# Forgetting attention: plain f32 matmuls replaced by three rounded products of high and low parts

## The chip, the cores and the metric

The kernel runs on one core of a Trainium2 chip. The metric is device time in microseconds (us), the median of several runs. One run of the same program is also taken with the hardware profiler; its page and its trace are what is read here.

## What is computed

Two network blocks on a sequence of 512 tokens of width 1024, all in f32. The first block has two layers; the first of these is the one that is changed here. It projects the input to queries, keys and values of 12 heads of width 128, and attends causally, with a forget gate that adds a bias to each score:

```python
s = jnp.einsum('bhqd,bhkd->bhqk', qi, k).astype(jnp.float32) * scale
s = s + ci[..., None] - c[:, :, None, :]
mask = key_pos[None, :] <= qpos[:, None]
s = jnp.where(mask[None, None], s, NEG)
p = jax.nn.softmax(s, axis=-1).astype(v.dtype)
return jnp.einsum('bhqk,bhkd->bhqd', p, v)
```

Around it stand a cross attention with 4 heads over 256 memory rows, a gate `silu(z)` and an output projection. The second layer replaces the forgetting attention by retention. The second block (dilated attention, a convolution, a gated feed forward part) is not touched.

## The kernel before

Each engine has its own instruction stream, written by hand in the order in which it runs; engines wait for each other by semaphores (`x.wait_ge(semaphore, value)`). Nothing is scheduled by a planner.

**Two kinds of matmul.** A projection (`products`, L1845 to L1852) splits both its operands: weights and activations are rounded to fp32r ("high", `whi`, `Hh`), and what the rounding lost is rounded again ("low", `wlo`, `Hl`). Each 128-row chunk is then three matmuls on rounded operands, high times high, high times low and low times high, 128 x 512 each; a block has 8 chunks. The matmuls inside the attention (L1936 for the scores, L1969 for the weighted values) take plain f32 operands. TensorE runs each plain f32 matmul of the program as two MATMUL instructions, so the 48 of L1936 stand in the trace as 96. A transpose (L1952) is one.

**Weights.** SyncE loads a block of weights of 512 KB into one of 4 slots (L457), when the block four places earlier has been used. ScalarE rounds it (`whi`, L665), GpSimd subtracts (`wlo`, L531).

**The forgetting layer.** After the block for the forget gate and the first head's three blocks (q, k, z), 12 blocks (`val0`, L2094 to L2096) make the values of all heads, in three groups of four PSUM banks. ScalarE scales each bank and keeps it in `values` (`keep_values`, L831). Then there is one turn for each head i = 1 to 11 (`softmax_turn("fox", ...)`), each of about 22 us. TensorE runs in a turn:

1. `fox_scores` of head i-1: four matmuls, query block 0 to 3 against 128, 256, 384 and 512 keys, into the banks A0 to A3;
2. the q block and the k block of head i (`products`, 24 matmuls each);
3. `turn_probs`: 10 transposes of the probabilities of head i-1, again into A0 to A3;
4. the z block of head i; ahead of its fifth chunk (`c == 4`) stands `weigh_values` of head i-1: four matmuls of 512, 384, 256 and 128 columns, added up in the bank PV.

VectorE runs in a turn: the softmax of head i-1 (L1296 to L1313), q and k of head i out of PSUM (L1352, L1354), `head_out` (the weighted values times the gate, L1328, L1330, L1332), z of head i (L1357). ScalarE runs: the rounding of one block of weights, the exponentials (L740), the rounding of a second block, the copy of the transposed probabilities to `probsT` (L747, four copies), the rounding of a third block, tanh of z. The scores of head 11 and its weighted values stand in the first turn of the cross attention (`mem0`), where the weighted values come behind the fourth block.

## Time and profile before

| | us |
|---|---|
| median of 3 runs | 1866.2 |
| lowest, highest | 1865.28, 1867.84 |
| span of the profiled execution | 1865.8 |

The page of the profile gives busy time by engine, shares of the span in 40 slices, the chain of work that ended last, and groups of instructions by line. "PE" is TensorE's matmul, "PEld" its weight load, DVE is VectorE, ACT ScalarE, POOL GpSimd. Matmuls are pipelined: one that is shown as 0.39 us long may start 0.23 us after the one before it. What a matmul costs is therefore read from the distance of starts in the timeline, and not from its duration. Times in the timeline are from the start of the span.

### The profile page before, as it was taken

The numbers are of one execution on the slowest core, as the hardware profiler recorded it, in microseconds if no ns is written. First come the engines' busy times: TensorE is split into PE (matmuls) and PEld (weight loads), VectorE is DVE, ScalarE is ACT, GpSimd is POOL, SyncE is SP. The second block draws the span as 40 slices with busy tenths as digits, with TensorE's granted clock in tenths as the row PEclk, the third lists the DMA queues.
The fourth block names the chain that finished last, engine by engine and source line by source line (L and its number), as shares of the span: only waits on it lengthen the run. The fifth ranks groups of instructions, "written<-read, shape, count | busy, mean of one in ns | idle before, by whom it ended". The sixth has DMA issues, their size and how long they took to land.

```text
span 1865.8 us, 23617 instructions
## 1 busy us (share of the span) xinstructions
PE 1832.0 (98%) x8424; PEld 1498.3 (80%) x8424; DVE 847.1 (45%) x1494; ACT 735.5 (39%) x1159; POOL 786.2 (42%) x376
## 2 busy tenths in 40 slices
PE   8999999999999999999999999997999899999998
PEld 6887777888888777888888888885888678888887
DVE  5024334453110555534249988946333464455202
ACT  5333333333333565543343233347233374444313
POOL 3443344444444333443444444353444454444442
PEclk9999999999999999999999999999999999999999
DMA  5333332333333323333333433331333323333332
GB/s 169 109 85 86 90 90 80 91 96 90 91 96 108 101 80 91 89 92 90 96 96 91 108 95 80 80 79 44 92 101 102 90 76 92 92 101 91 112 96 96
DMA packets 293549, 174.20 MB, mean 93 GB/s; under 512 B 16368, under 2 KB 280072, under 8 KB 293472
## 3 DMA queue, kind: packets, MB, share of 16 engines
q1 hardware_dynamic: 280528, 165.17, 31.1%
q0 software_dynamic: 2448, 7.93, 1.7%
q10 hardware_dynamic: 10496, 0.07, 0.3%
q8 instruction: 49, 0.80, 0.2%
q14 instruction: 28, 0.23, 0.1%
HBM read 170.95 MB, written 2.20 MB: 93 GB/s over the span
## 4 chain that ended last, share of the span: by engine, by line
PE 93%; DMA 2%; DVE 2%; ACT 2%; issue 0%; POOL 0%; SPq 0%; DVEq 0%; ACTq 0%; POOLq 0%
PE proj L1849 22%; PE proj L1851 22%; PE proj L1850 22%; PE A L1936 1%; PE PV L1969 1%; PE A L2094 1%; PE A L2096 1%; PE A L2095 1%; PE A L2376 1%; PE A L2374 1%; PE A L2375 1%; DMA wraw<-w_in 1%; PE PV L1973 1%; PE A L1942 1%; PE A L1952 1%; PE A L2032 1%
## 5 line engine op out<-in xcount | busy, mean ns | idle before, releaser
L531 POOL TENSOR_TENSOR wlo<-wraw,whi 128x1024 fp32r<-128x1024 f32 (+1 forms) x305 | 723.2, 2373 | 1006.8 <-ACT whi L665 1006.3
L665 ACT ACTIVATE whi<-wraw 128x1024 fp32r<-128x1024 f32 (+1 forms) x304 | 318.5, 1048 | 770.0 <-DMA wraw<-w_in 179.0
L1849 PE MATMUL proj<-Hh,whi 128*128 128x512 f32 x1448 | 581.5, 402 | 0.5 <-DVE uv L1785 0.3
L1851 PE MATMUL proj<-Hh,wlo 128*128 128x512 f32 x1448 | 565.6, 391 | 0.0
L1850 PE MATMUL proj<-Hl,whi 128*128 128x512 f32 x1448 | 565.0, 390 | 0.0
L1849 PEld LDWEIGHTS proj<-Hh,whi 128*128 128x128 f32 x1448 | 272.6, 188 | 61.4 <-issue 4.3
L1850 PEld LDWEIGHTS proj<-Hl,whi 128*128 128x128 f32 x1448 | 272.7, 188 | 59.5 <-issue 5.0
L1851 PEld LDWEIGHTS proj<-Hh,wlo 128*128 128x128 f32 x1448 | 272.3, 188 | 58.0
L1532 DVE SCALAR_TENSOR_TENSOR A<-cin,dwT,A 128x512 f32<-128x512 f32 x232 | 175.1, 755 | 6.8
L1849 PE MATMUL proj<-Oh,whi 128*128 128x512 f32 x256 | 101.1, 395 | 0.8 <-DVE Ol L1332 0.8
L1850 PE MATMUL proj<-Ol,whi 128*128 128x512 f32 x256 | 99.7, 389 | 0.0
L1851 PE MATMUL proj<-Oh,wlo 128*128 128x512 f32 x256 | 99.7, 389 | 0.0
L1849 PEld LDWEIGHTS proj<-Oh,whi 128*128 128x128 f32 x256 | 48.1, 188 | 11.6 <-DVE Ol L1332 1.2
L1850 PEld LDWEIGHTS proj<-Ol,whi 128*128 128x128 f32 x256 | 48.1, 188 | 10.2 <-issue 0.5
L1851 PEld LDWEIGHTS proj<-Oh,wlo 128*128 128x128 f32 x256 | 48.0, 188 | 10.1
L1444 DVE TENSOR_TENSOR X<-X,proj 128x512 f32 (+1 forms) x16 | 11.0, 688 | 92.1 <-PE proj L1851 92.1
L1785 DVE TENSOR_TENSOR uv<-proj,rms 128x512 f32<-128x512 f32 x21 | 14.5, 692 | 81.8 <-PE proj L1851 81.8
L1328 DVE SCALAR_TENSOR_TENSOR ob<-PV,gate 128x512 f32<-128x512 f32 x20 | 13.8, 692 | 82.7 <-PE PV L1969 59.8
L1823 DVE TENSOR_TENSOR VT<-VT,gains 128x512 f32<-128x512 f32 x1 | 0.7, 700 | 101.2 <-ACT sq L1181 101.2
L756 ACT ACTIVATE ztanh<-z 128x512 f32<-128x512 f32 x20 | 12.6, 630 | 68.1 <-DVE z L1357 50.5
L1309 DVE RECIPROCAL small<-small 128x4 f32<-128x4 f32 x20 | 3.6, 178 | 77.3 <-ACT probs L740 77.3
L1668 DVE TENSOR_TENSOR sq<-proj,rms 128x512 f32<-128x512 f32 x16 | 11.1, 692 | 59.5 <-PE proj L1851 55.9
(440 smaller groups left out, 2799.5 us busy)
## 6 DMA issues: line engine op xcount, KB each, us to landing
wraw<-w_in SPq DMA_DIRECT2D x68, 512.0 KB, 3.8
wraw<-fox_w_in SPq DMA_DIRECT2D x57, 512.0 KB, 3.7
wraw<-ret_w_in SPq DMA_DIRECT2D x44, 512.0 KB, 3.8
wraw<-w_up SPq DMA_DIRECT2D x44, 512.0 KB, 3.8
wraw<-w_out SPq DMA_DIRECT2D x40, 512.0 KB, 4.0
wraw<-w_down SPq DMA_DIRECT2D x22, 512.0 KB, 3.6
wraw<-w_mem_kv SPq DMA_DIRECT2D x16, 512.0 KB, 4.1
wraw<-conv_pw_w SPq DMA_DIRECT2D x8, 512.0 KB, 4.0
```

Source lines behind the costliest of these rows:

```text
L531: pool.tensor_tensor(wlo[s][:, 0:r, :], wraw[s][:, 0:r, :], whi[s][:, 0:r, :].bitcast(F32), ALU.subtract).then_inc(w_lo, 1)
L665: f(whi[s][:, 0:r, :], wraw[s][:, 0:r, :], ACT.Copy).then_inc(w_hi, 1)
L1532: ins = stt(conv_sum if tap < CONV - 1 else C[:, c, :], cin[:, c, tap:tap + S], dwT[:, c * CONV + tap:c * CONV + tap + 1], conv_sum, ALU.m ...
L1849: mm(dst, whi[s][:, c, :], xh, start=(first and c == 0), stop=False)
L1850: mm(dst, whi[s][:, c, :], xl, start=False, stop=False)
L1851: ins = mm(dst, wlo[s][:, c, :], xh, start=False, stop=(last and c == chunks - 1))
L1936: mm(A[i][:, 0:w], q[:, i * P:(i + 1) * P], k[:, 0:w], start=True, stop=True).then_inc(scores, 1)
L1942: mm(A[j][:, 0:NMEM], qm[:, j * P:(j + 1) * P], km, start=True, stop=True).then_inc(scores, 1)
L1952: ins = pe.transpose(A[j][:, (i - j) * P:(i - j + 1) * P], probs[:, FOXAT[i] + j * P:FOXAT[i] + (j + 1) * P], ident[:])
L1969: ins = mm(PV[:, j * P:S], values[:, u, j * P:(j + 1) * P], probsT[:, TRI[j]:TRI[j] + S - j * P], start=(j == 0), stop=(j == NT - 1))
L1973: ins = mm(PV[:], vtok[0][:, j, :], probsT[:, j * S:(j + 1) * S], start=(j == 0), stop=(j == MT - 1))
L2032: ins = mm(ret_sum[e][:, j * P:S], values[:, r, j * P:(j + 1) * P], decayed[e][:, TRI[j]:TRI[j] + S - j * P], start=(j == 0), stop=(j == N ...
```

## The change

In the 12 heads of the forgetting layer, every operand of the scores and of the weighted values is held as a high and a low part in fp32r, and each plain f32 matmul becomes three rounded ones. One stays: the scores of query block 0 (128 x 128). The high parts of q, k and of the probabilities are made by ScalarE (the copy to `probsT` writes `probs_high` in its stead), the low parts by VectorE. The values are kept as `Oh` and `Ol`, in place of `values`. Then `weigh_values` stands ahead of the seventh chunk of the z block instead of the fifth. The two tables `rcos` and `rsin` of the retention are loaded behind the cross attention, not at the start, since `probs_low` lies over them.

The core of the diff:

```diff
+        q_high, k_high, q_low = r_high[0], r_high[1], r_low[1]
...
@@ -547,8 +562,6 @@
                         split("val0", 0, b)
                     pool.wait_ge(b_out, 2)
                     pool.dma_start(b_dram, bias_rows[:]).then_inc(b_stored, 16)
-                    pool.dma_start(rcos[:], t["c_cos"]).then_inc(in_rope, 16)
-                    pool.dma_start(rsin[:], t["c_sin"]).then_inc(in_rope, 16)
                     pool.wait_ge(c_ready, 1)
                     pool.dma_start(c_dram, f_b).then_inc(c_stored, 16)
                     pool.wait_ge(c_stored, 16)
@@ -588,6 +601,9 @@
             for i in range(1, HEADS):
                 fox_turn(i)
             turns("mem0")
+            pool.wait_ge(pv_done, HEADS)
+            pool.dma_start(rcos[:], t["c_cos"]).then_inc(in_rope, 16)
+            pool.dma_start(rsin[:], t["c_sin"]).then_inc(in_rope, 16)
             turns("wo0")
             for b in range(HEADS):
                 split("val1", 0, b)
@@ -744,7 +760,9 @@
                 act.wait_ge(turned, u + 1)
                 if kind == "fox":
                     for j in range(NT):
-                        ins = f(probsT[:, TRI[j]:TRI[j] + S - j * P], A[j][:, 0:S - j * P], ACT.Copy)
+                        ins = f(probs_high[:, TRI[j]:TRI[j] + S - j * P], A[j][:, 0:S - j * P], ACT.Copy)
+                        if j < NT - 1:
+                            ins.then_inc(p_high, 1)
                 else:
                     for j in range(MT):
                         ins = f(probsT[:, j * S:(j + 1) * S], A[j][:], ACT.Copy)
@@ -762,6 +780,11 @@
             FOXW, FOXAT = [P * (i + 1) for i in range(NT)], [0, 128, 384, 768]
             MEMW, MEMAT = [NMEM] * NT, [NMEM * i for i in range(NT)]
 
+            def high_of(i, b):
+
+                act.wait_ge(evac, PH["fox"].g(i, b) + 1)
+                f((q_high, k_high)[b][:], (q, k)[b][:], ACT.Copy).then_inc(qk_high_made, 1)
+
             def softmax_turn(name, i, u, before):
 
                 if before == "ret":
@@ -770,6 +793,8 @@
                     split(name, i, 0, i)
                     exps(u - 1, FOXW, FOXAT)
                     split(name, i, 1, i)
+                    high_of(i, 0)
+                    high_of(i, 1)
                     copy_probsT(u - 1, before)
                     split(name, i, 2, i)
                     z_and_v(name, i, u)
@@ -828,7 +853,8 @@
                         act.wait_ge(v_summed[L], (NT - 1) * group + j + 1)
                     else:
                         act.wait_ge(w_used, PH["val" + str(L)].n(0, 4 * group + 3) + 1)
-                    f(kept_values(group, j), v_banks[L][group][j][:].rearrange("p (h n) -> p h n", h=4), ACT.Identity,
+                    to = kept_values(group, j) if L else split_values(group, j)[0]
+                    f(to, v_banks[L][group][j][:].rearrange("p (h n) -> p h n", h=4), ACT.Identity,
                       scale=(x_roots, v_roots)[L][:, j:j + 1]).then_inc(v_kept[L], 1)
 
             def value_turns(L):
@@ -839,6 +865,9 @@
                     if L == 0 and b < 2:
                         for c in range(4 * b, 4 * b + 4):
                             mem_high(c)
+                    if L == 0 and b == 2:
+                        high_of(0, 0)
+                        high_of(0, 1)
                 keep_values(L, 2)
 
             def ret_finish(i):
@@ -1283,6 +1312,35 @@
             for c in range(KC):
                 mem_low(c)
 
+            def low_of(i, b):
+
+                dve.wait_ge(qk_high_made, 2 * i + b + 1)
+                tt((q_low, k_low)[b][:], (q, k)[b][:], (q_high, k_high)[b][:].bitcast(F32), ALU.subtract).then_inc(qk_low_made, 1)
+
+            def low_values(group):
+
+                for j in range(NT):
+                    high, low = split_values(group, j)
+                    dve.wait_ge(v_kept[0], NT * group + j + 1)
+                    stt(low, v_banks[0][group][j][:].rearrange("p (h n) -> p h n", h=4), x_roots[:, j:j + 1],
+                        high.bitcast(F32), ALU.mult, ALU.subtract).then_inc(v_low, 1)
+
+            def low_probs(u):
+
+                for j in range(NT):
+                    if j < NT - 1:
+                        dve.wait_ge(p_high, (NT - 1) * u + j + 1)
+                    else:
+                        dve.wait_ge(probs_out, u + 1)
+                    at = slice(TRI[j], TRI[j] + S - j * P)
+                    ins = tt(probs_low[:, at], A[j][:, 0:S - j * P], probs_high[:, at].bitcast(F32), ALU.subtract)
+                ins.then_inc(p_low, 1)
+
+            low_of(0, 0)
+            low_of(0, 1)
+            for group in range(GROUPS):
+                low_values(group)
+
             def softmax(u, widths, at):
 
                 if widths is FOXW:
@@ -1352,6 +1410,9 @@
                     stt(q[:], proj[ph.bank(0, i)][:], SCALE, rms[:], ALU.mult, ALU.mult).then_inc(evac, 1)
                     arrived(name, i, 1)
                     tt(k[:], proj[ph.bank(1, i)][:], rms[:], ALU.mult).then_inc(evac, 1)
+                    low_of(i, 0)
+                    low_of(i, 1)
+                    low_probs(u - 1)
                     head_out(u - 1, head)
                     arrived(name, i, 2)
                     tt(z[0][:], proj[ph.bank(2, i)][:], rms[:], ALU.mult).then_inc(evac, 1)
@@ -1365,6 +1426,8 @@
                 dve.tensor_copy(vT[:, 0:NMEM], proj[ph.bank(2)][:, 0:NMEM]).then_inc(evac, 1)
                 if before in ("fox", "mem") and not late:
                     head_out(u - 1, head)
+                if late:
+                    low_probs(u - 1)
                 arrived(name, i, 3)
                 tt(z[0][:], proj[ph.bank(3)][:], rms[:], ALU.mult).then_inc(evac, 1)
                 if late:
@@ -1929,11 +1992,14 @@
             def fox_scores(u):
 
 
-                pe.wait_ge(evac, PH["fox"].g(u, 1) + 1)
-                since(pe, probs_out, u)
-                for i in range(NT):
-                    w = P * (i + 1)
-                    mm(A[i][:, 0:w], q[:, i * P:(i + 1) * P], k[:, 0:w], start=True, stop=True).then_inc(scores, 1)
+                pe.wait_ge(qk_low_made, 2 * u + 2)
+                since(pe, p_low, u)
+                mm(A[0][:, 0:P], q[:, 0:P], k[:, 0:P], start=True, stop=True).then_inc(scores, 1)
+                for i in range(1, NT):
+                    to, at, w = A[i][:, 0:P * (i + 1)], slice(i * P, (i + 1) * P), P * (i + 1)
+                    mm(to, q_high[:, at], k_high[:, 0:w], start=True, stop=False)
+                    mm(to, q_high[:, at], k_low[:, 0:w], start=False, stop=False)
+                    mm(to, q_low[:, at], k_high[:, 0:w], start=False, stop=True).then_inc(scores, 1)
 
             def mem_scores(name, i, u):
                 pe.wait_ge(evac, PH[name].g(i, 1) + 1)
@@ -1959,15 +2025,19 @@
                 ins.then_inc(turned, 1)
 
             def weigh_values(u, kind):
-                pe.wait_ge(probs_out, u + 1)
-                if kind == "mem":
+                if kind == "fox":
+                    pe.wait_ge(p_low, u + 1)
+                else:
+                    pe.wait_ge(probs_out, u + 1)
                     pe.wait_ge(v_out, u - HEADS + 1)
 
                 since(pe, o_done, u)
                 if kind == "fox":
                     for j in range(NT):
-                        ins = mm(PV[:, j * P:S], values[:, u, j * P:(j + 1) * P], probsT[:, TRI[j]:TRI[j] + S - j * P],
-                                 start=(j == 0), stop=(j == NT - 1))
+                        to, of, at = PV[:, j * P:S], slice(j * P, (j + 1) * P), slice(TRI[j], TRI[j] + S - j * P)
+                        mm(to, Oh[:, u, of], probs_high[:, at], start=(j == 0), stop=False)
+                        mm(to, Oh[:, u, of], probs_low[:, at], start=False, stop=False)
+                        ins = mm(to, Ol[:, u, of], probs_high[:, at], start=False, stop=(j == NT - 1))
                 else:
                     for j in range(MT):
                         ins = mm(PV[:], vtok[0][:, j, :], probsT[:, j * S:(j + 1) * S], start=(j == 0), stop=(j == MT - 1))
@@ -1987,11 +2057,11 @@
                 if name == "fox":
                     fox_scores(u - 1)
                     if i == 1:
-                        pe.wait_ge(v_kept[0], HEADS)
+                        pe.wait_ge(v_low, HEADS)
                     products(name, i, 0, 0, H, par=i)
                     products(name, i, 1, 1, H, par=i)
                     turn_probs(u - 1, before)
-                    products(name, i, 2, 2, H, par=i, each=lambda c: weigh_values(u - 1, before) if c == 4 else None)
+                    products(name, i, 2, 2, H, par=i, each=lambda c: weigh_values(u - 1, before) if c == 6 else None)
                     return
                 if before == "fox":
                     fox_scores(u - 1)
@@ -2105,7 +2175,7 @@
                 if b == 4:
                     pe.wait_ge(mem_lo, KC)
                 if b == 8:
-                    pe.wait_ge(v_kept[0], 4)
+                    pe.wait_ge(v_low, 4)
                 values_of(0, b)
                 if b == 0:
                     pe.wait_ge(mem_scaled, MT)
@@ -2116,7 +2186,7 @@
                     for x in range(4, KC):
                         pe.wait_ge(mem_lo, x - 3)
                         turn_mem(x)
-            pe.wait_ge(v_kept[0], 8)
+            pe.wait_ge(v_low, 8)
             for i in range(1, HEADS):
                 softmax_turn("fox", i, i, "fox")
 
```

**On TensorE, the weighted values of one head and the scores of the next.** In a row before, the four matmuls of the weighted values, in the middle of the z block, and the four of the scores, between two blocks:

```order
L1969 MATMUL PV<-probsT,values 128x512 [waits o_done,probs_out]
L1969 MATMUL PV<-probsT,values 128x384
L1969 MATMUL PV<-probsT,values 128x256
L1969 MATMUL PV<-probsT,values 128x128
...
L1936 MATMUL A<-k,q 128x128 [waits probs_out,evac]
L1936 MATMUL A<-k,q 128x256
L1936 MATMUL A<-k,q 128x384
L1936 MATMUL A<-k,q 128x512
```

and now:

```order
L2038 MATMUL PV<-probs_high,Oh 128x256
L2039 MATMUL PV<-probs_low,Oh 128x256
L2040 MATMUL PV<-probs_high,Ol 128x256
L2038 MATMUL PV<-probs_high,Oh 128x128
L2039 MATMUL PV<-probs_low,Oh 128x128
L2040 MATMUL PV<-probs_high,Ol 128x128
...
L1997 MATMUL A<-k,q 128x128 [waits p_low,qk_low_made]
L2000 MATMUL A<-r_high 128x256
L2001 MATMUL A<-k_low,r_high 128x256
L2002 MATMUL A<-r_high,r_low 128x256
```

Eight plain matmuls have become one plain and 21 rounded ones. (`r_high` is the name under which q_high and k_high lie, `r_low` that of q_low.)

**On VectorE, between k of a head and the output of the head before.** Before:

```order
L1354 TENSOR_TENSOR k<-proj,rms 128x512 [waits w_used]
L1328 SCALAR_TENSOR_TENSOR ob<-PV,gate 128x512 [waits gated,pv_done]
L1330 CAST Oh<-ob 128x512 [waits o_done]
L1332 TENSOR_TENSOR Ol<-ob,Oh 128x512 [waits dve_own]
```

and now:

```order
L1412 TENSOR_TENSOR k<-proj,rms 128x512 [waits w_used]
L1318 TENSOR_TENSOR r_low<-q,r_high 128x512 [waits qk_high_made]
L1318 TENSOR_TENSOR k_low<-k,r_high 128x512 [waits qk_high_made]
L1336 TENSOR_TENSOR probs_low<-A,probs_high 128x512 [waits p_high]
L1336 TENSOR_TENSOR probs_low<-A,probs_high 128x384 [waits p_high]
L1336 TENSOR_TENSOR probs_low<-A,probs_high 128x256 [waits p_high]
L1336 TENSOR_TENSOR probs_low<-A,probs_high 128x128 [waits probs_out]
L1386 SCALAR_TENSOR_TENSOR ob<-PV,gate 128x512 [waits gated,pv_done]
```

Six subtractions have come in between; the first two wait for ScalarE's rounding of q and k, the next three for a copy of the probabilities each, and the sixth for the last copy (`probs_out`).

**On ScalarE, at the same place.** Before:

```order
L665 ACTIVATE whi<-wraw 128x1024 [waits w_used,w_landed0]
L747 ACTIVATE probsT<-A 128x512 [waits turned]
L747 ACTIVATE probsT<-A 128x384
L747 ACTIVATE probsT<-A 128x256
L747 ACTIVATE probsT<-A 128x128
L665 ACTIVATE whi<-wraw 128x1024 [waits w_used,w_landed1]
```

and now:

```order
L681 ACTIVATE whi<-wraw 128x1024 [waits w_used,w_landed0]
L786 ACTIVATE r_high<-q 128x512 [waits evac]
L786 ACTIVATE r_high<-k 128x512 [waits evac]
L763 ACTIVATE probs_high<-A 128x512 [waits turned]
L763 ACTIVATE probs_high<-A 128x384
L763 ACTIVATE probs_high<-A 128x256
L763 ACTIVATE probs_high<-A 128x128
L681 ACTIVATE whi<-wraw 128x1024 [waits w_used,w_landed1]
```

The rounding of q and of k stands between the rounding of a block of weights and the four copies of the probabilities, which are the same as before but for the tile they write.

## Rows read from the trace of the kernel before

**Rows 1.** The page: busy us, share of the span, instructions; and the chain.

```profile
PE 1832.0 (98%) x8424; PEld 1498.3 (80%) x8424; DVE 847.1 (45%) x1494; ACT 735.5 (39%) x1159; POOL 786.2 (42%) x376
...
PE 93%; DMA 2%; DVE 2%; ACT 2%; issue 0%; POOL 0%; SPq 0%; DVEq 0%; ACTq 0%; POOLq 0%
```

**Rows 2.** Waits, 100 to 360 us (who <- for whom: total, times, longest).

```profile
PEld proj L1849 <- ACT values L831: 0.5, 1, 0.5
```

**Rows 3.** The turns of the heads: busy us (PE PEld DVE ACT POOL), granted clock.

```profile
110.00:352.00 242.00, 242.00 (x1087) 191.51 (x1087) 98.43 (x313) 83.12 (x180) 100.08 (x56) 1.00 0.32 84
```

**Rows 4.** Timeline, TensorE, scores of one head: start, length, engine, instruction.

```profile
219.47 2.32 PE L1936 MATMUL A<-k,q 128*128 128x128 f32 x8
...
221.87 0.40 PE L1850 MATMUL proj<-Hl,whi 128*128 128x512 f32 x1
```

**Rows 5.** Timeline, TensorE, transposes and weighted values of a head.

```profile
210.72 1.25 PE L1952 MATMUL A<-ident,probs 128*128 128x128 f32 x10
...
212.05 0.39 PE L1850 MATMUL proj<-Hl,whi 128*128 128x512 f32 x1
...
214.57 2.32 PE L1969 MATMUL PV<-probsT,values 128*128 128x512 f32 x8
...
216.95 0.39 PE L1850 MATMUL proj<-Hl,whi 128*128 128x512 f32 x1
```

**Rows 6.** Timeline, TensorE, first and last of 48 rounded matmuls of 256 columns.

```profile
358.16 0.28 PE L1849 MATMUL proj<-Mh,whi 128*128 128x256 f32 x1
...
363.79 0.28 PE L1851 MATMUL proj<-Mh,wlo 128*128 128x256 f32 x1
```

**Rows 7.** Timeline, end of the value blocks: ScalarE keeps, TensorE goes on.

```profile
110.28 2.32 PE L1936 MATMUL A<-k,q 128*128 128x128 f32 x8
110.37 0.68 ACT L831 ACTIVATE values<-PV,small 128x512 f32<-128x512 f32 x1
...
110.94 1.27 ACT L831 ACTIVATE values<-proj,small 128x512 f32<-128x512 f32 x2
...
112.67 0.39 PE L1850 MATMUL proj<-Hl,whi 128*128 128x512 f32 x1
```

**Rows 8.** Timeline, turn 6: k ends, rounding, copies, weighted values.

```profile
232.33 0.39 PE L1851 MATMUL proj<-Hh,wlo 128*128 128x512 f32 x1
...
232.84 1.06 ACT L665 ACTIVATE whi<-wraw 128x1024 fp32r<-128x1024 f32 x1 [6.04 <-DMA wraw<-fox_w_in]
...
233.85 1.43 ACT L747 ACTIVATE probsT<-A 128x512 f32<-128x512 f32 x4
...
236.18 0.41 PEld L1969 LDWEIGHTS PV<-probsT,values 128*128 128x128 f32 x2
...
236.41 2.32 PE L1969 MATMUL PV<-probsT,values 128*128 128x512 f32 x8
```

**Rows 9.** Timeline, turn 7, the same places.

```profile
254.98 1.06 ACT L665 ACTIVATE whi<-wraw 128x1024 fp32r<-128x1024 f32 x1 [6.46 <-DMA wraw<-fox_w_in]
...
258.25 2.32 PE L1969 MATMUL PV<-probsT,values 128*128 128x512 f32 x8
```

**Rows 10.** Timeline, VectorE, turn 6: z, three softmax steps, normalising.

```profile
219.67 0.69 DVE L1357 TENSOR_TENSOR z<-proj,rms 128x512 f32<-128x512 f32 x1 [0.45 <-PE proj L1851]
...
220.49 0.29 DVE L1296 CUSTOM_DVE_ANT_0 probs<-A,decay 128x128 f32<-128x128 f32 x1
...
221.12 0.42 DVE L1296 CUSTOM_DVE_ANT_0 probs<-A,decay 128x256 f32<-128x256 f32 x1
...
221.98 0.56 DVE L1296 CUSTOM_DVE_ANT_0 probs<-A,decay 128x384 f32<-128x384 f32 x1 [0.21 <-PE A L1936]
...
227.04 1.36 DVE L1313 TENSOR_SCALAR probs<-probs,small 128x128 f32<-128x128 f32 x4
```

**Rows 11.** Timeline, GpSimd, end of the cross attention, start of the output projection.

```profile
434.64 2.38 POOL L531 TENSOR_TENSOR wlo<-wraw,whi 128x1024 fp32r<-128x1024 f32 x1 [1.44 <-ACT whi L665]
442.22 2.41 POOL L531 TENSOR_TENSOR wlo<-wraw,whi 128x1024 fp32r<-128x1024 f32 x1 [5.20 <-ACT whi L665]
```

More of the change, by code:

```diff
@@ L174, in build @@
             probs = sb("probs", [P, 1280], F32, one)
+            with ExitStack() as halves:
+                probs_high = sb("probs_high", [P, 1280], F32R, halves)
             probsT = sb("probsT", [P, 1280], F32, one)
-            z = [sb(f"z{e}", [P, S], F32, one) for e in range(2)]
-            gate = [sb(f"gate{e}", [P, S], F32, one) for e in range(2)]
+            z0, gate0 = sb("z0", [P, S], F32, one), sb("gate0", [P, S], F32, one)
+            with ExitStack() as halves:
+                k_low = sb("k_low", [P, S], F32R, halves)
+            z1 = sb("z1", [P, S], F32, one)
+            with ExitStack() as halves:
+                probs_low = sb("probs_low", [P, 1280], F32R, halves)
+            gate1 = sb("gate1", [P, S], F32, one)
+            rcos = sb("rcos", [P, S], F32, one)
+            rsin = sb("rsin", [P, S], F32, one)
+            z, gate = (z0, z1), (gate0, gate1)
             with ExitStack() as squared:
@@ L182, in build @@
             decay = [sb(f"decay{e}", [P, S], F32, one) for e in range(2)]
-            rcos = sb("rcos", [P, S], F32, one)
-            rsin = sb("rsin", [P, S], F32, one)
             mean_r = sb("mean_r", [P, P], F32R, one)
@@ L298, in build @@
         turned, probs_out, pv_done, o_done = sem("turned"), sem("probs_out"), sem("pv_done"), sem("o_done")
+        qk_high_made, qk_low_made, p_high, p_low, v_low = (sem(x) for x in ("qk_high_made", "qk_low_made", "p_high", "p_low", "v_low"))
         v_turned, v_out, z_tanh, gated = sem("v_turned"), sem("v_out"), sem("z_tanh"), sem("gated")
@@ L439, in kept_values, with split_values @@
             return values[:, 4 * group:4 * group + 4, j * P:(j + 1) * P]
+        def split_values(group, j):
+            at = slice(4 * group, 4 * group + 4), slice(j * P, (j + 1) * P)
+            return Oh[:, at[0], at[1]], Ol[:, at[0], at[1]]
         block = ctx.enter_context(nc.Block())
```

## Prediction

> **What bounds the kernel now.** I read the page first: TensorE is busy for 98% of the span and is 93% of the chain that ended last [rows 1]. Then the waits over all the turns of the forgetting layer. In 260 us TensorE waits for another engine once, for 0.5 us, behind the values that ScalarE keeps [rows 2], and its clock is granted in full [rows 3], so 2.4 GHz. VectorE is busy for 98 of 242 us there and ScalarE for 83 [rows 3]. So the time of this layer is the sum of what TensorE's instructions cost, and the cost of one is the distance of starts in the timeline. The change has two faces: shorter groups on TensorE, and longer chains on ScalarE and VectorE behind which TensorE could begin to wait.
>
> **Prices.** (a) Rounded, 512 columns: from 221.87 to 232.33 there are 46 steps [rows 4, 8], 0.227 us each. (b) Rounded, 256 columns: 47 steps from 358.16 to 363.79 [rows 6], 0.120 us. Columns over 2.4 GHz are 0.213 and 0.107, so both carry the same 0.013 us extra, and 384 columns should take 0.173. (c) The scores of a head in plain f32: from 219.47 to the next block's start, which is 221.87 less one step of 0.227, are 2.17 us [rows 4]. The weighted values, 214.57 to 216.95 less 0.227, are 2.15 [rows 5]. Both are 1280 columns in two instructions each, so 4 cycles a column. (d) A plain 128-column instruction: 10 transposes from 210.72 to 212.05 less 0.227 are 1.10 us, 0.11 each [rows 5]; a plain 128 x 128 matmul is two, 0.22.
>
> The profile's 4 cycles a column agree with the Trainium skill, FP8 and Floating Point Precision, section TensorE Precision Notes: true FP32 takes four passes. By passes alone the new form would save a quarter, 0.53 us a group of 2.13, 12.8 us in 24 groups, and 1855.0 after the waits below. The rows say less, for each rounded matmul carries its 0.013.
>
> **Scores, 12 heads.** Now 0.22 for block 0, then 3 x (0.120 + 0.173 + 0.227) = 1.56, and 0.02 at the change of kind as in (c): 1.80 against 2.17. Gain 0.37 x 12 = 4.4 us.
>
> **Weighted values, 12 heads.** The three wide widths are 1.56 again. Then come three rounded matmuls of 128 columns, a shape that the trace does not show. Bounds: the line through (a) and (b) gives 0.067 each; a full plain matmul of that width is 0.22 each, which it would be if rounding brought nothing for narrow ones. Between them stands the nearest row, the 128-column instruction of the transposes with a weight load of its own, 0.11. I take 0.11, as no instruction with its own weight load comes faster in these rows. The group is then 1.56 + 0.33 = 1.89 against 2.15: gain 0.26 x 12 = 3.1 us. With 0.067 it is 0.13 a head more, with 0.22 it is 0.33 a head less, 4.0 us in all.
>
> The Trainium skill, TensorE: Matmul & The Clock Gate, section LDWEIGHTS, gives a load of 128 columns 107 ns; an estimate by it would put three narrow ones at 0.32, where the line of the rows has 0.20. No run here shows this shape yet.
>
> **Start of the turns: a new wait.** The last value is kept by 110.94 + 1.27 = 112.21, and the q block behind the first scores starts at 112.67 less 0.227 = 112.44 [rows 7], 0.23 after it, one weight load. Now VectorE must also make the last low part of the values. Its steps of 512 columns take 0.69 with 0.60 from start to start, as fast as ScalarE's 0.57 [rows 7, 10], so it ends one step later: 112.21 + 0.04 + 0.69 = 112.94, and q starts at 113.17. The first scores would be through at 110.28 + 1.80 = 112.08. TensorE loses 1.1 us, once. The first softmax begins 2 us later on VectorE; that is covered, since the normalised probabilities are there at 228.40 in turn 6 and wanted by the transposes at 232.56 [rows 8, 10], 4.2 us of slack.
>
> **The chain to the weighted values, 11 turns.** In turn 6, ScalarE rounds weights from 232.84 [rows 8], and an instruction hands over 0.10 before its end (110.37 to 110.94 for a length of 0.68 [rows 7]). So q is rounded from 233.80, k from 234.37, and the copies, 1.43 long in all, end at 236.37 instead of 235.28. VectorE takes k's low part from 235.04, then the four of the probabilities. Their widths cost 0.69, 0.56, 0.42 and 0.29, by z and by the softmax steps that also read a bank and SBUF [rows 10], each less 0.09 when in a row. They end at 237.33. The weighted values now stand two chunks later, 6 x 0.227: from 236.41 to 237.77, their weight load from 236.18 to 237.54 [rows 8]. Slack 0.21 us: the two chunks just about pay for the chain. In turn 7 the rounding starts at 254.98 and the weighted values at 258.25 [rows 9]: the chain of 4.49 ends at 259.47, the load is due at 259.38, late by 0.09. By the same working turn 1 is even, the others have 0.1 to 0.5, one 1.8. Since I built this chain out of eight neighbours' durations, I take 0.5 us in sum, with bounds of 0 and 3.
>
> **What costs nothing.** The low parts of q and k for the scores are ready by 235.6, the scores come at 241. The later `head_out` moves z's copy some 0.5 us back; its bank is wanted a whole block of 5.4 us later. The softmax starts 0.5 us later by it, within the 4.2 us. VectorE gets 1.3 + 2.0 us more a turn, ScalarE 1.2, in turns of 21.8, at busy shares of 41% and 34% [rows 3]. In the first turn of the cross attention the weighted values come a whole block behind the transposes, which covers the chain. The tables' load moves into a hole of 5.2 us on GpSimd [rows 11]: two issues, and 0.5 MB beside a weight block that is used three blocks later. Where it stood before, TensorE waited for no weights.
>
> **Sum.** 4.4 + 3.1 - 1.1 - 0.5 = 5.9 us. The profiled execution's 1865.8 becomes 1859.9; it lies 0.4 under the median, so 1860.3.
>
> **Rivals.**
> - *Narrow rounded matmuls are dear.* Three at 0.22 eat up the gain of the weighted values: 0.66 + 1.56 = 2.22 against 2.15. Then 5.9 - 4.0 = 1.9 us are left: 1864.3, which can't be told from no change. For it: nothing in the trace is rounded and narrower than 256 columns, so nothing excludes it. Against it: (a) and (b) show rounded matmuls at one cycle a column at either width.
> - *They are as cheap as the line says.* 1.5 us more: 1858.8. Against it: there is no start-to-start distance under 0.11 here with a fresh weight load; but none was asked for by a rounded one.
> - *The chain comes late and the change costs time.* The place is the first weight load of the weighted values, which waits for `p_low`. ScalarE's two roundings stand between a landing weight block and the copies, and VectorE's low parts of q and k stand ahead of those of the probabilities. Each 0.1 us of lateness costs 1.1 us. With the other terms at 6.4, the sum is zero at 0.6 us late in each of 11 turns, and slower by 0.2% at 0.9 us. It takes a weight block that lands 1 us later in a turn, or 0.12 us more on each of eight instructions. At 1 us late: 1866.2 - 6.4 + 11 = 1870.8. Against it: the landing hangs on TensorE's own blocks and moves with them; in turns 6 and 7 it lies 0.28 and 0.58 behind k's end [rows 8, 9].
>
> **How the numbers follow.** Forecast 40% (1860.3), dear narrow ones 28% (1864.3), cheap ones 18% (1858.8), a late chain 14%: 3% still faster, 5% with the gain gone, 6% slower. A measurement of this kernel can tell about 0.2%, 3.7 us, from no change: faster means under 1862.5. Faster: 0.40 + 0.18 + 0.03 = 0.61; same: 0.28 + 0.05 = 0.33; slower 0.06. The range goes from 1857.8, the cheap case with no wait, to 1865.0, the dear case with half a us of extra waits.
>
> **What would show it.** In the profile of the changed kernel: scores of 1.80 us from their first start to the next block; weighted values of 1.89, and the starts of their last three at 0.11, 0.067 or 0.22; one wait of about 1 us ahead of the q block at 112; 0 to 0.1 us a turn ahead of the weighted values, by VectorE. Wrong would be: a wait in every turn at that place, a wait of the scores, or a turn that is longer though its groups are shorter.

## The result, and the profile after

| | kernel before | changed kernel |
|---|---|---|
| time, median (lowest to highest) | 1865.74 us (1862.6 to 1867.84, 4 runs) | 1887.64 us (1885.44 to 1888.39, 4 runs) |
| ratio to before, 95% interval | | 1.0115 (1.0101 to 1.0128) |
| span of the profiled execution | 1865.8 us | 1885.6 us |
| one turn of the heads (mean of 11) | 21.84 us | 23.64 us |

The change costs 1.15%, where I had forecast a gain of 0.3%. The page of the changed kernel, busy times and the chain by engine, against [rows 1]:

```profile
PE 1833.5 (97%) x8508; PEld 1510.9 (80%) x8508; DVE 909.0 (48%) x1578; ACT 747.5 (40%) x1183; POOL 793.8 (42%) x376
...
PE 86%; DVE 5%; DMA 4%; ACT 3%; issue 1%; POOL 0%; SPq 0%; DVEq 0%; ACTq 0%; POOLq 0%
```

The busy shares hardly move. The chain does: TensorE's share falls from 93% to 86%, VectorE's rises from 2% to 5%. So something on VectorE now sets the pace for a part of the time. TensorE's waits in the turns of the heads, where [rows 2] had one of 0.5 us (total, times, longest):

```profile
PE PV L2038 <- DVE probs_low L1336: 19.3, 11, 2.2
...
PE proj L1912 <- DVE Ol L1325: 1.1, 1, 1.1
```

In every one of the 11 turns TensorE stands ahead of the weighted values until VectorE has made the low part of the probabilities, 1.75 us each time. Measured from the first matmul of a head's scores to the next head's, a turn was 21.84 us, eleven times (240.2 us). It is now 23.91, 23.01, 22.95, 23.16, 25.07, 23.39, 23.73, 24.92, 23.36, 23.45 and 23.05 (260.0 us). The eleven turns are taken off the spans, and 1625.6 us are left of either (1865.8 - 240.2 and 1885.6 - 260.0). So the whole loss, 19.8 us, lies in the turns.

Turn 6 of the changed kernel, the chain to the weighted values (timeline of all engines; compare [rows 8]):

```profile
241.17 1.06 ACT L681 ACTIVATE whi<-wraw 128x1024 fp32r<-128x1024 f32 x1 [5.17 <-DMA wraw<-fox_w_in]
...
242.13 0.62 ACT L786 ACTIVATE r_high<-q 128x512 fp32r<-128x512 f32 x1
242.31 2.40 POOL L546 TENSOR_TENSOR wlo<-wraw,whi 128x1024 fp32r<-128x1024 f32 x1 [5.53 <-ACT whi L681]
...
242.65 0.62 ACT L786 ACTIVATE r_high<-k 128x512 fp32r<-128x512 f32 x1
...
242.78 2.48 DVE L1318 TENSOR_TENSOR r_low<-q,r_high 128x512 fp32r<-128x512 f32 x1 [0.54 <-ACT r_high L786]
...
243.18 1.40 ACT L763 ACTIVATE probs_high<-A 128x512 fp32r<-128x512 f32 x4
...
244.68 1.74 POOL L582 TENSOR_TENSOR decay<-decay,sq 128x512 f32<-128x512 f32 x1
...
245.18 1.78 DVE L1318 TENSOR_TENSOR k_low<-k,r_high 128x512 fp32r<-128x512 f32 x1
...
246.43 2.76 POOL L546 TENSOR_TENSOR wlo<-wraw,whi 128x1024 fp32r<-128x1024 f32 x1
...
246.89 1.67 DVE L1336 TENSOR_TENSOR probs_low<-A,probs_high 128x512 fp32r<-128x512 f32 x4
...
248.61 0.50 PE L2038 MATMUL PV<-probs_high,Oh 128*128 128x512 f32 x1 [1.90 <-DVE probs_low L1336]
```

ScalarE is as forecast: its copies of the probabilities end 3.41 us after the rounding of the weights begins (forecast: 236.37 less 232.84, 3.53). VectorE is not. The low part of q takes 2.48 us and that of k 1.78, where I had 1.3 for the two together. The four low parts of the probabilities behind them take 1.67 together (forecast 1.69), although a subtraction of GpSimd runs beside them too.

The reader should look at the ends rather than at the lengths. The low part of q ends at 245.26, which is 0.55 after GpSimd's `wlo` (242.31 + 2.40 = 244.71). That of k ends at 246.96, 0.54 after GpSimd's addition into `decay` (244.68 + 1.74 = 246.42). That addition was issued while q's low part ran; alone it takes 1.28, here 1.74, and 245.26 + 1.28 is 0.12 more than its end. These are not two engines that share something and both get slower. Each time, the one that comes second does its work when the first has ended: VectorE's 0.69 us end 0.55 behind GpSimd, so all but about 0.14 of them lie behind it.

### The profile page after: what moved, and what is told of

Read it like the earlier page. It is cut to its first block, busy times and chain, and to the rows that moved or that the text cites. A ratio compares the mean times of both kernels' runs of the same rounds, so it can differ in the third digit from the quotient of the medians.

```text
span 1885.6 us, 23893 instructions
## 1 busy us (share of the span) xinstructions
PE 1833.5 (97%) x8508; PEld 1510.9 (80%) x8508; DVE 909.0 (48%) x1578; ACT 747.5 (40%) x1183; POOL 793.8 (42%) x376
## 4 chain that ended last, share of the span: by engine, by line
PE 86%; DVE 5%; DMA 4%; ACT 3%; issue 1%; POOL 0%; SPq 0%; DVEq 0%; ACTq 0%; POOLq 0%
PE proj L1912 21%; PE proj L1914 20%; PE proj L1913 20%; DMA wraw<-fox_w_in 2%; PE A L2164 1%; PE A L2165 1%; PE A L2166 1%; DVE r_low L1318 1%; PE A L2444 1%; PE A L2446 1%; PE A L2445 1%; DVE k_low L1318 1%; ACT whi L681 1%; DVE probs_low L1336 1%; PE PV L2043 1%
```

## The experiments

Theory A: VectorE's subtractions with both inputs in SBUF (`q`, `r_high`; `k`, `k_high`) cannot run beside a GpSimd instruction that reads SBUF, and the low parts of the probabilities stand behind them. Rival B: the chain is simply longer than its slack, whatever runs on GpSimd. Rival C: the wait is only half of the loss, and the other half is in the new shapes on TensorE or in its clock. All edits are made to the changed kernel. Each ratio below is to the kernel before, in runs on the same chip.

### 1. The low parts of the probabilities first

```diff
                     tt(k[:], proj[ph.bank(1, i)][:], rms[:], ALU.mult).then_inc(evac, 1)
+                    low_probs(u - 1)
                     low_of(i, 0)
                     low_of(i, 1)
-                    low_probs(u - 1)
```

> The changed kernel with one exchange on VectorE: the low parts of the probabilities are made ahead of the low parts of q and k, not behind them. Theory A (an instruction of VectorE with both inputs in SBUF stands still while GpSimd subtracts; one with an input in PSUM does not): the low parts of the probabilities end about 1 us before the weighted values are due, the wait of about 1.9 us in each of 11 turns is gone, and the kernel takes 1860 to 1863 us (q's and k's low parts now come close to the next scores). Rival B (the chain of roundings, copies and subtractions is too long by itself, whatever its order): at least 1 us of wait stays in a turn, 1875 us or more. Rival C (the loss lies in the rounded matmuls or the clock, not in the wait): 1887 us as now.

Measured: 1859.92 us (1857.82 to 1862.67, 6 runs; before 1866.15 in 20), ratio 0.997 (0.9958 to 0.9983). There is no wait ahead of the weighted values any more, and a turn is 21.19 us. VectorE and GpSimd in turn 6:

```profile
231.67 1.13 DVE L1318 TENSOR_TENSOR r_low<-q,r_high 128x512 fp32r<-128x512 f32 x1
...
232.72 0.68 DVE L1318 TENSOR_TENSOR k_low<-k,r_high 128x512 fp32r<-128x512 f32 x1
...
232.96 2.71 POOL L546 TENSOR_TENSOR wlo<-wraw,whi 128x1024 fp32r<-128x1024 f32 x1 [0.71 <-ACT whi L681]
```

The loss is gone with the place of two calls in VectorE's order, and no instruction is left out. The turn was forecast at 21.84 - 0.37 - 0.26 = 21.21, so both gains on TensorE are real. What VectorE does ahead of `low_probs` cost the 20 us, not what TensorE now executes. It does not tell A from B yet, since this order takes the two low parts out of the chain whatever they last. But the other direction of A is seen here: k's low part comes first and takes its 0.68, and GpSimd's `wlo`, which starts 0.24 later, takes 2.71 instead of 2.40. Nor are the two low parts quick in this order: q's lasts 1.13 behind GpSimd's addition (231.67), and in two turns k's meets `wlo` and lasts 2.88, longer than in the changed kernel. These turns take 21.19 us like the others, since nobody waits for k's low part there.

### 2. GpSimd reads nothing beside them

In the turns of the heads after the first, GpSimd fills `wlo` with zeros and does not subtract, so the low part of those weights is left out of the product.

```diff
                 pool.wait_ge(w_hi, n + 1)
+                if name == "fox" and i:
+                    pool.memset(wlo[s][:, 0:r, :].bitcast(F32), 0.0).then_inc(w_lo, 1)
+                    return
                 pool.tensor_tensor(wlo[s][:, 0:r, :], wraw[s][:, 0:r, :], ...
```

> The changed kernel, but in the head turns GpSimd fills the low part of the weights with zeros instead of subtracting (the low part of these weights is left out of the result). Its order and its waits stay, it only reads nothing from SBUF in these 33 instructions. Theory A: the low parts of q and k take 0.69 us each instead of 2.48 and 1.78, except where they meet the 1.3 us that GpSimd adds the mask; the wait of a turn falls from 1.9 us to between 0 and 1, 1860 to 1872 us. Rival B (GpSimd has nothing to do with it, the subtractions are slow since q and its high part are read together, or because ScalarE and TensorE read beside them): both stay at 2.5 and 1.8 us, and the time at 1887 us.

Measured: 1859.02 us (1857.77 to 1861.37, 8 runs), ratio 0.9964 (0.9953 to 0.9974). One wait of 0.5 us is left ahead of the weighted values. Turn 6 (lines are three higher, by the edit):

```profile
231.18 0.95 POOL L547 MEMSET wlo<- 128x1024 f32 x1 [6.21 <-ACT whi L684]
...
231.84 0.68 DVE L1321 TENSOR_TENSOR r_low<-q,r_high 128x512 fp32r<-128x512 f32 x1
...
232.09 1.58 POOL L585 TENSOR_TENSOR decay<-decay,sq 128x512 f32<-128x512 f32 x1
232.62 1.61 DVE L1321 TENSOR_TENSOR k_low<-k,r_high 128x512 fp32r<-128x512 f32 x1
```

This tells A from B. VectorE's order and TensorE's are those of the changed kernel, only GpSimd's instruction is another, and q's low part is back at 0.68 (median of 12: 0.681), though the fill overlaps it by 0.29. In the ten turns in which it follows the fill, the overlap is 0.15 to 0.46 us and the length never over 0.69. So a GpSimd instruction that only writes does not hold it up. k's low part still meets the addition and ends at 234.23, 0.56 after that one's end at 233.67. It is the same law with another partner.

### 3. q's parts early, k's still ahead of the probabilities

```diff
+                    high_of(i, 0)
                     split(name, i, 1, i)
-                    high_of(i, 0)
...
+                    low_of(i, 0)
                     arrived(name, i, 1)
                     tt(k[:], proj[ph.bank(1, i)][:], rms[:], ALU.mult).then_inc(evac, 1)
-                    low_of(i, 0)
```

> The changed kernel, with q rounded and its low part made right behind q, in a stretch in which GpSimd is idle; k's low part still stands ahead of the probabilities' and still meets GpSimd's subtraction. Theory A: q's low part takes 0.69 us; k's waits for the end of GpSimd's instruction and then takes 0.6 more; the probabilities' end some 0.6 us late, 0.5 to 0.8 us of wait in a turn, 1865 to 1869 us. Rival B (the number of instructions in the chain counts, 0.7 us each): two instructions of 1.2 us in sum are out of the chain, the wait falls from 1.9 to 0.7 us: nearly the same time, but k's low part takes 0.69 us and starts late. The durations tell them apart, the time does not.

Measured: 1863.06 us (1859.49 to 1866.83, 10 runs), ratio 0.999 (0.9978 to 1.0001). Turns are 21.3 to 22.1 us. Turn 6, and the wait over all turns:

```profile
227.79 0.69 DVE L1318 TENSOR_TENSOR r_low<-q,r_high 128x512 fp32r<-128x512 f32 x1 [0.70 <-ACT r_high L786]
...
230.29 2.39 POOL L546 TENSOR_TENSOR wlo<-wraw,whi 128x1024 fp32r<-128x1024 f32 x1 [5.21 <-ACT whi L681]
...
231.28 1.96 DVE L1318 TENSOR_TENSOR k_low<-k,r_high 128x512 fp32r<-128x512 f32 x1 [0.70 <-ACT r_high L786]
```

```profile
PE PV L2038 <- DVE probs_low L1336: 2.3, 7, 0.6
```

q's low part now runs where GpSimd is idle and takes 0.69. k's is the one that meets `wlo`, and its end is 233.24, again 0.56 after GpSimd's (232.68). The wait shrinks from 19.3 to 2.3 us in sum. That is less than the 0.5 to 0.8 a turn that I expected, and so is the time (1865 to 1869). At the weight load the wait is longer, as the load is due before the matmul: 6.5 us in sum or 0.59 a turn, against 23.9 in the changed kernel. The turns tell a little more than the waits do: they are longer than those of the next experiment by 0.46 us each (239.42 less 234.39, over 11), with 0.21 of it in the waits. Another 0.2 is what a late group costs beside the counted wait (0.3 in each of 7), which is taken up under "What the 20 us are".

### 4. Both moved: the order that the chain wants

q's parts early as in 3; of k, ScalarE's rounding behind the copies of the probabilities, and VectorE's low part behind theirs.

```diff
+                    high_of(i, 0)
                     split(name, i, 1, i)
-                    high_of(i, 0)
-                    high_of(i, 1)
                     copy_probsT(u - 1, before)
+                    high_of(i, 1)
...
+                    low_of(i, 0)
                     arrived(name, i, 1)
                     tt(k[:], proj[ph.bank(1, i)][:], rms[:], ALU.mult).then_inc(evac, 1)
-                    low_of(i, 0)
-                    low_of(i, 1)
                     low_probs(u - 1)
+                    low_of(i, 1)
```

> Both: q's high and low parts behind q, where GpSimd is idle, and k's high and low parts behind the copies and low parts of the probabilities. Theory A: no wait ahead of the weighted values, none ahead of the scores (k's low part is ready 1 us or more before them, even blocked), turns of 21.2 us instead of 21.84 before: 1859 to 1861 us, the forecast of the prediction without its 0.5 us. Rival B: with only the copies and four subtractions left in the chain this should be free of waits too, so it doesn't tell A from B; it tells what the shorter groups on TensorE are worth: if the gain of 7.5 us less 1.1 is not there, the prices were wrong.

Measured: 1859.69 us (1855.14 to 1860.09, 5 runs), ratio 0.9953 (0.9936 to 0.9969). Ten turns of 21.19 us and the first, with the wait at its start, of 22.50. VectorE and GpSimd:

```profile
231.55 2.40 POOL L546 TENSOR_TENSOR wlo<-wraw,whi 128x1024 fp32r<-128x1024 f32 x1 [5.77 <-ACT whi L681]
...
232.41 1.68 DVE L1336 TENSOR_TENSOR probs_low<-A,probs_high 128x512 fp32r<-128x512 f32 x4 [1.03 <-ACT probs_high L763]
...
233.91 1.29 POOL L582 TENSOR_TENSOR decay<-decay,sq 128x512 f32<-128x512 f32 x1
234.01 1.73 DVE L1318 TENSOR_TENSOR k_low<-k,r_high 128x512 fp32r<-128x512 f32 x1
```

Here both sides of the law stand in four rows. The low parts of the probabilities lie inside GpSimd's subtraction but for their last 0.14 us, and neither side takes longer than alone: 2.40 for GpSimd, and 1.68 against 1.67 in turn 6 of experiment 2, where no subtraction of GpSimd is beside them. Their first input is a bank of PSUM. k's low part has two inputs in SBUF; it starts 0.10 after the addition, the addition keeps its 1.29, and k's low part ends 0.54 after it. It still takes 1.73 us; only nobody waits for it now.

In the same profile, TensorE without a wait shows the prices of the new groups (weighted values from 235.69, scores from 238.97):

```profile
235.69 0.39 PE L2038 MATMUL PV<-probs_high,Oh 128*128 128x512 f32 x1
...
237.26 0.22 PE L2038 MATMUL PV<-probs_high,Oh 128*128 128x128 f32 x1
237.32 0.28 PE L2039 MATMUL PV<-probs_low,Oh 128*128 128x128 f32 x1
237.43 0.27 PE L2040 MATMUL PV<-probs_high,Ol 128*128 128x128 f32 x1
...
237.82 0.40 PE L1913 MATMUL proj<-Hl,whi 128*128 128x512 f32 x1
...
238.97 0.38 PE L1997 MATMUL A<-k,q 128*128 128x128 f32 x2
...
240.77 0.39 PE L1912 MATMUL proj<-Hh,whi 128*128 128x512 f32 x1
```

Scores: 1.80 us, forecast 1.80. Weighted values: 237.82 less one step of 0.227, less 235.69, are 1.90; forecast 1.89. The three narrow rounded matmuls take 0.33 in all (237.26 to 237.59), so 0.11 each, with starts 0.06 and 0.11 apart at first: the nearest row was the right price, and neither rival on the narrow ones came.

### 5. The start of the turns

Experiment 4, and the last group of values takes its banks in another order, so that q's bank is among the first to be read out; TensorE then waits for ten low parts, not twelve.

```diff
-        v_banks = ((others, A, others), (A, others, A))
+        v_banks = ((others, A, (*proj, VT, PV)), (A, others, A))
...
-                        pe.wait_ge(v_low, HEADS)
+                        pe.wait_ge(v_low, 2 * NT + 2)
```

> The reordered kernel (e4) with the third group of values laid into the banks in another order: the two that the next q and k blocks write come first, so that TensorE waits for 10 of the 12 low parts of the values instead of all. The prediction put 1.1 us on this wait, and e4 shows 1.0. If that is its whole cause, the wait is gone and nothing takes its place, since q would start behind the scores at about the time at which the tenth low part is ready (within 0.2 us): 0.8 to 1.0 us under e4, so 1858.7 to 1859. If VectorE's first softmax, which begins behind the twelfth as before, becomes late for the first transposes, the gain is given back: the time of e4.

Measured: 1855.06 us (1854.55 to 1859.71, 5 runs; before 1866.59 in 9), ratio 0.9945 (0.9931 to 0.9959). The first turn is 21.20 us instead of 22.50. It starts thus:

```profile
107.43 1.41 DVE L1325 SCALAR_TENSOR_TENSOR Ol<-proj,small,Oh 128x512 fp32r<-128x512 f32 x2 [19.15 <-ACT Oh L857]
...
108.76 0.74 DVE L1325 SCALAR_TENSOR_TENSOR Ol<-VT,small,Oh 128x512 fp32r<-128x512 f32 x1
...
108.99 0.40 PE L1912 MATMUL proj<-Hh,whi 128*128 128x512 f32 x1
```

The two low parts of the `proj` banks are made by 108.84, and q's block follows the scores with no wait. The changed kernel has the same places with a wait of 1.07:

```profile
112.10 1.40 DVE L1325 SCALAR_TENSOR_TENSOR Ol<-proj,small,Oh 128x512 fp32r<-128x512 f32 x2
...
113.56 0.49 PE L1912 MATMUL proj<-Hh,whi 128*128 128x512 f32 x1 [1.07 <-DVE Ol L1325]
```

That was forecast as 1.1, once, so this term held. This kernel is faster than the kernel before and the changed one. The turn accounts for 1.3 us against experiment 4. Most of the remaining 3.3 us between the two medians is not owed to the edit: in the profiled executions the first scores start at 107.2 here and at 110.5 in experiment 4. The other profiles fall on one side or the other too: 107.6 to 107.9 in experiments 1, 3 and 6, 110.0 to 110.5 in the kernel before, both profiles of the changed kernel and experiment 2.

Most of that difference arises in the first 16 us. In the profile of experiment 4, two rounded matmuls of 512 columns start 0.42 us apart (13.76 and 14.18), which is one column a cycle at 1.2 GHz. Here the same two are 0.24 apart (12.87 and 13.11), at 2.4 GHz. From 12 to 15 us TensorE does 22 or 23 matmuls in the four profiles with the early scores and 12 or 13 in the five with the late ones. (The column of the granted clock has 1.00 in both, so it is the steps that tell.) Why the fast level comes some 5 us later in some executions stays open. The times of whole runs carry this difference of about 3 us in their starts, the lengths of the turns do not. Experiment 4's own runs fall in two groups, 1855.1 to 1855.3 and 1859.7 to 1860.1, and those of experiment 5 in 1854.6 to 1855.2 and one of 1859.7. Group by group their means differ by 0.3 us or less, so the 1.3 us of the first turn are shown by the trace and not by the times.

### 6. The weighted values one chunk later

The wait alone is made shorter: TensorE does three more matmuls, 0.68 us, ahead of the group.

```diff
-                    products(..., each=lambda c: weigh_values(u - 1, before) if c == 6 else None)
+                    products(..., each=lambda c: weigh_values(u - 1, before) if c == 7 else None)
```

> The changed kernel with the weighted values one chunk (0.68 us) further back in the z block. If the low parts come at a fixed time behind k, and TensorE stands idle until then, each turn is 0.68 us shorter: 11 x 0.68 = 7.5 us, from 1887.6 to 1880. If the wait moves along with TensorE's place, nothing changes. If the long turns (25.1 and 24.9 us against 23.3 of the others), in which the granted clock fell, come from the length of the wait, they are gone too, another 3.4 us: 1876.7.

Measured: 1876.15 us (1872.36 to 1877.15, 4 runs), ratio 1.0049 (1.0033 to 1.0064), 11.5 us less than the changed kernel. The wait over all turns, and the clock of all turns (the last columns of the window are granted clock, DMA share, GB/s):

```profile
PE PV L2038 <- DVE probs_low L1336: 12.8, 11, 1.3
```

```profile
110.00:365.00 255.00, 241.44 (x1179) 201.72 (x1180) 156.99 (x392) 94.74 (x206) 106.84 (x56) 1.00 0.30 81
```

The turns are 250.4 us in sum, 9.6 less than in the first profile of the changed kernel. The waits give 6.5 of it (19.3 less 12.8), 0.59 a turn. The other 3.1 are the two long turns, which are not there: none is over 22.8 us but the first, 23.88. Of the 11.5 us, the rest is mostly the start: this profile's first scores come at 107.6, those of the changed kernel at 110.5.

### 7. The changed kernel again

> The changed kernel once more, on the chip of the two others. In its first profile two turns of the eleven took 25.07 and 24.92 us where the others took 23.0 to 23.9, and the granted clock was lower in these two. If something in those turns causes it, the same two are long again. If it is the clock that falls behind a wait of 2 us in some turns and not in others, other turns, or another number of them, are long. Time 1885 to 1889 us either way.

Measured: 1887.8 us (1883.78 to 1888.63, 4 runs), ratio 1.0109 (1.0093 to 1.0124): the result stands. The turns are 24.39, 23.47, 23.26, 23.31, 23.19, 25.30, 23.57, 23.39, 23.23, 25.20 and 23.51 us. Its waits, and the stretch with the sixth turn:

```profile
PE PV L2038 <- DVE probs_low L1336: 21.1, 11, 2.3
```

```profile
228.00:252.00 24.00, 21.73 (x100) 18.21 (x100) 12.96 (x34) 8.35 (x18) 9.76 (x5) 0.93 0.28 77
```

There are two long turns again, but the sixth and tenth, not the fifth and eighth. So they aren't tied to a place in the program.

### The long turns

In the first profile of the changed kernel, the stretch with the fifth turn and the one behind it:

```profile
205.00:228.00 23.00, 20.95 (x95) 17.46 (x94) 12.17 (x32) 8.20 (x18) 9.70 (x5) 0.93 0.30 80
228.00:252.00 24.00, 22.10 (x109) 18.45 (x108) 14.15 (x36) 8.34 (x18) 9.75 (x5) 1.00 0.29 77
```

And TensorE in the former, from the wait on:

```profile
223.69 0.50 PE L2038 MATMUL PV<-probs_high,Oh 128*128 128x512 f32 x1 [2.05 <-DVE probs_low L1336]
...
224.98 0.53 PE L2039 MATMUL PV<-probs_low,Oh 128*128 128x384 f32 x1
225.30 0.53 PE L2040 MATMUL PV<-probs_high,Ol 128*128 128x384 f32 x1
225.62 0.42 PE L2038 MATMUL PV<-probs_high,Oh 128*128 128x256 f32 x1
```

384 columns are 0.32 us apart, which is one column a cycle at 1.2 GHz; without the wait they are 0.17 apart. A turn less its wait is 21.46 to 21.49 us in eight of the eleven turns (the first, with the start wait, 22.84); in the fifth and eighth it is 23.02 and 23.04. The low clock therefore costs 1.55 us each time. It came in 4 of the 22 turns of the two profiles, behind waits of 2.05, 1.88, 2.27 and 2.16 us; others as long (2.25, 2.11) were not followed by it, and none of the 11 waits up to 1.33 of experiment 6 was. What decides within the long ones stays open.

## Why the prediction was wrong

**TensorE's terms held.** Scores 1.80 us (forecast 1.80), weighted values 1.90 (1.89), narrow rounded matmuls 0.11 each (0.11, nearest row), a turn without a wait 21.19 (21.21). The start wait is 1.07 (1.1). Experiments 1, 2 and 4, with no wait ahead of the weighted values or one of 0.5 us, come to 1859.9, 1859.0 and 1859.7, where the forecast for the changed kernel was 1860.3. It is the time of a kernel whose low parts of the probabilities are not held up (and the start of the program alone moves these times by 3 us, so the agreement is no finer than that). One sum of the range is off: the cheap case with no wait is 1860.3 - 1.5 - 0.5 = 1858.3, not 1857.8. It changes nothing here.

**The step that failed** is in "The chain to the weighted values": "VectorE takes k's low part from 235.04, then the four of the probabilities". It prices the low parts of q and k at 0.69 and 0.60 us, by z and the softmax steps, rows that read a PSUM bank and one SBUF operand. The low parts of q and k read two SBUF operands. I treated duration as a matter of width alone, and looked on VectorE for neighbours, not on GpSimd for what runs at that moment. The trace of before had both: GpSimd in turn 6, and a place where VectorE reads `ob` in SBUF. The second block is that of the last turn.

```profile
233.98 2.40 POOL L531 TENSOR_TENSOR wlo<-wraw,whi 128x1024 fp32r<-128x1024 f32 x1 [6.39 <-ACT whi L665]
236.35 1.27 POOL L569 TENSOR_TENSOR decay<-decay,sq 128x512 f32<-128x512 f32 x1
```

```profile
347.49 2.40 POOL L531 TENSOR_TENSOR wlo<-wraw,whi 128x1024 fp32r<-128x1024 f32 x1 [0.66 <-ACT whi L665]
...
348.69 1.49 DVE L1330 CAST Oh<-ob 128x512 fp32r<-128x512 f32 x1
...
350.21 0.69 DVE L1332 TENSOR_TENSOR Ol<-ob,Oh 128x512 fp32r<-128x512 f32 x1
```

The cast, 0.43 alone, takes 1.49 and ends 0.29 after GpSimd's subtraction; the subtraction with two SBUF inputs behind it, GpSimd being idle by then, takes 0.69. It is so in every turn: the 11 casts last 0.75 to 2.28 us and end 0.28 or 0.29 behind a GpSimd subtraction. The subtractions behind them all take 0.69, so the row with the same kind of operands would still have given the wrong price: one has to look at what runs on GpSimd. The Trainium skill, SBUF — State Buffer, section SBUF: two separate sides, says it outright: a VectorE operation with two SBUF inputs and a GpSimd operation that reads SBUF need the same pair of ports, the first to start holds it for its whole length, and the other is blocked fully. The traces here agree: in the profiles of the changed kernel and of experiments 1 to 5, the 80 low parts of q and k that took longer than 0.75 us all started while a GpSimd subtraction or addition ran, and ended 0.54 to 0.56 us behind its end; the others took 0.68 or 0.69.

**The chain with this law.** By the rows of before alone: `wlo` ends at 236.38, q's low part at 236.38 + 0.55 = 236.93. The addition, issued at 236.35, is held until then, less the 0.12 read above, and ends at 236.93 + 1.28 - 0.12 = 238.09. k's low part ends at 238.09 + 0.55 = 238.64, the four of the probabilities 1.60 later (246.96 to 248.56 above), at 240.24. The weight load is due at 237.54: 2.7 us late, where I had 0.21 early. In the changed kernel the weight block lands 0.45 us sooner after k's last matmul (0.06 to the start of the rounding against 0.51 in [rows 8]), which leaves 2.25. The weight load there waited 2.33.

**The rival that came** is the late chain, which had 14% and was priced for 1 us of lateness, at 1870.8. Its place was right, and so, nearly, were its price and its threshold. Both were reckoned from when the weight load is due. The loads of the changed kernel were 23.9 us late in sum and cost 22.5 (25.6 less 3.1 for the clock, see below). In experiment 3 they were 0.59 us late a turn, and the turns took 239.4 us against 240.2 before: the gain was all but gone, as forecast for 0.6. I held it to need a later weight block or 0.12 us more on each of eight instructions, and did not see that two instructions alone could bring 3 us. What I left out besides is that the clock can fall behind such a wait.

**What the 20 us are.** The turns of the changed kernel last 260.0 us, those of experiment 4 234.4, a difference of 25.6. Waits are 19.3 of it. A wait is counted from the end of the last matmul, which is 0.39 long (246.32 to 246.71 in turn 6), while with no wait the next one starts 0.227 after it: 0.16 more each, 1.8 in eleven. Behind a wait the first step is 0.34 instead of 0.227 (248.61 to 248.95), and the group and the step behind it last 0.14 more than in experiment 4 (248.61 to 250.88, against 235.69 to 237.82): 1.5. The low clock adds 2 x 1.55 = 3.1. The sum is 25.7. Against the kernel before, TensorE gains 240.2 - 234.4 = 5.8 us in the turns, and 25.6 - 5.8 = 19.8 is the loss.

**What was costed at nothing.** The scores never waited for the low parts, and no wait for the tables' load shows among TensorE's waits, so those steps held. The later z cost one wait of 0.2 us, behind the turns. "VectorE gets 1.3 + 2.0 us more a turn" did not hold: from 110 to 365 us it is busy for 149.9 us, against 103.8 before, which is 13.9 a turn against 8.9, since the time for which it is blocked counts as busy. And it is the order, not the share of 41%, that decided.

## What to carry to other kernels

Price a new instruction by a row with the same places of its operands (PSUM or SBUF), and look up what GpSimd does at the moment at which it will run: a short VectorE subtraction in SBUF can last as long as the rest of GpSimd's instruction and then 0.55 us more, nearly its own length. Where a chain must have such steps, put those that nobody waits for behind those that TensorE waits for; one place in the order was worth 25.6 us in the eleven turns here. And a slack of 0.2 us that is the difference of sums of eight borrowed durations is no slack: its range must be the range of those durations under what runs beside them.

## What the runs showed of the hardware

- A VectorE subtraction of 512 columns with both inputs in SBUF takes 0.69 us beside an idle GpSimd. Beside a GpSimd subtraction or addition that started earlier it ends 0.55 us after that one's end (2.48 us long in the changed kernel, up to 2.88 in experiment 1). The other way round GpSimd is the one that gets longer: its addition 1.28 to 1.74, its subtraction 2.40 to 2.76.
- A cast of 512 columns within SBUF takes 0.43 alone and is held up as well: in the 11 turns of the kernel before it lasts 0.75 to 2.28 us and ends 0.28 or 0.29 behind GpSimd's subtraction.
- With one input in PSUM, neither gets longer (1.68 and 2.40 side by side in experiment 4; 1.67 with no subtraction beside it in experiment 2). Nor does q's low part beside a GpSimd fill that only writes (0.68).
- Three rounded matmuls of 128 columns, each with a weight load of its own, take 0.33 us, 0.11 each on the average (single steps of 0.06 to 0.16). Plain transposes take 0.11 each too.
- TensorE's granted clock fell to the level of 1.2 GHz behind 4 of 22 waits of 1.07 to 2.27 us (the four: 1.88 to 2.27), at 1.55 us each, and behind none of 11 waits of 0.94 to 1.33. At the start of the program it reached 2.4 GHz before 12 us in four profiles and at 15 to 16.5 us in five.
- A TensorE wait costs 0.3 us more than the profile counts: 0.16 by where it is counted from, 0.14 by the restart.
